# Prompt attention with values on column halves, and sample attention with cached rows turned by VectorE and scores on 16 tiles

## The chip, the core and the metric

The kernel runs on one core of one Trainium2 chip. The metric is the device time of one execution in microseconds (us); three runs were timed before. 

## The reference

One inference step of two decoder layers, in fp32, for 512 prompt tokens and for 8 sample sequences of 4 new tokens each, whose 4096 past positions lie in a paged cache. In each layer a combined projection feeds four branches; one of them is latent attention with 8 heads, a latent width of 128 and a rotary width of 32. Then come gates, a merge, a layer norm and a mixture of 16 experts. The part that matters here, shortened:

```python
def mla_attend(q_lat, q_rope, ckv, krope, q_pos, k_pos):
    s = einsum('bthc,blc->bhtl', q_lat, ckv) + einsum('bthr,blr->bhtl', q_rope, krope)
    s = where(q_pos >= k_pos, s * (QK_NOPE + QK_ROPE) ** -0.5, -1e30)
    return einsum('bhtl,blc->bthc', softmax(s, axis=-1), ckv)

lat = mla_attend(q_lat, q_rope, concat([past_ckv, ckv]), concat([past_krope, krope]), pos, k_pos)
c_out = einsum('bthc,chv->bthv', lat, w_uv)
```

For the samples the past keys are `cache_ckv[l, page_table]` (128 wide) and `cache_krope[l, page_table]` (32 wide).

## The kernel before

Each layer runs five stages one after the other, each a block with its own program for every engine: `project`, `attend` (prompt attention, behind a run of small products), `attend_sample`, `merge` and `experts`. Inside a block each engine works through its instructions in the order of the code and waits on semaphores; `due(k, sem, n)` is the count n of a semaphore within the layer. A new block starts when all engines have left the last one.

**`attend`.** The units of `B_UNITS` (L568) are small products on TensorE, each into one of four pairs of PSUM banks, and are taken from there by the engine named behind the colon (A ScalarE, D VectorE). The last, `qdr`, puts the rotary sample queries of 4 sequences on the diagonal of `qbd` (L779 to L784). Then 16 turns follow: a query block of 128 tokens (4) times a pair of heads (4). In turn i of block qb = i // 4, TensorE makes two score tiles over (qb + 1) x 128 keys (`scores`, L911, K = 96); VectorE adds the causal mask to the last 128 columns (L806), takes the maximum (L808) and makes the bias (L810); ScalarE takes the exponentials (L695). Two turns later TensorE turns the probabilities (`turn`, L938) and ScalarE copies them (L703); three turns later `values` (L928) multiplies, with the turned probabilities (128 columns) as the stationary side and 64 columns of V streaming. At the end of a block VectorE divides by the sums (`block_out`, L795), TensorE turns the 512 columns (`block_turn`, L944) and VectorE keeps them in `cc` (`block_keep`, L800). TensorE's order is scores(i), values(i-3), turn(i-2). Each fp32 product appears as two matmuls in the trace (two passes), a transpose as one.

**`attend_sample`.** 8 sequences are two halves of 4. A step s (of 8) is one half's 4 batches with 1024 keys each; partition r of a batch holds 8 consecutive cached rows. `load_cache` (L564, L565) fetches for each batch first the rotary rows (128 x 256) and then the latent rows (128 x 1024) by indirect DMA on GpSimd, with a semaphore each, into one of `BUFS` = 3 buffers. Steps 0 to 2 are loaded in `attend`. For the steps behind them the GpSimd program is:

```python
pool.wait_ge(*due(k, k.d_pv, 2 * (s - BUFS) + 2))
load_cache(k, pool, s, range(0, 2))
...
pool.wait_ge(*due(k, k.d_pv, 2 * (s - BUFS) + 3))
load_cache(k, pool, s, range(2, 4))
```

A step is worked in two units of 512 keys per batch. For a unit GpSimd lines up the rotary rows (L985); TensorE makes 4 transposes of them (L1010) and 16 of the latent rows (L1018), which VectorE and ScalarE copy out (L1137, L1140, L1098); then one rotary product with `qbd` and four latent products on column quarters (L1026, L1030) give the scores. VectorE takes the maximum (L1169 to L1173), ScalarE the exponentials (L1106); TensorE turns the probabilities (L1038), ScalarE copies them (L1114), and 32 matmuls on column quarters make the value product (L1047), after which `d_pv` counts one. VectorE adds it to the running output (L1153). TensorE's order is scores(u), values(u-1), turn(u+1), turn_probs(u). The new tokens' own keys are worked before unit 0 (L1055 to L1070, L1122 to L1146). SyncE fetches the first weights of `merge` once `d_pv` has reached 12. The stages that follow begin at L1254.

## Time and profile before

| | us |
|---|---|
| median of three runs | 1947.16 |
| lowest, highest | 1941.71, 1953.26 |
| span of the profiled execution | 1919.0 |
| its own total time | not recorded; the median is 28.2 above the span |
| TensorE busy | 1776.3 (93%) |
| VectorE busy | 801.3 (42%) |
| ScalarE busy | 444.7 (23%) |
| GpSimd busy | 372.1 (19%) |

Busy time is the time in which an engine had an instruction at work. TensorE's matmuls are pipelined, so a matmul's own length (for instance 0.60 us for 512 columns) is longer than the spacing of two of them. PEclk is the granted clock of TensorE as a share of 2.4 GHz; at 0.50 it is 1.2 GHz.

### The profile page before, as it was taken

How to read it: one execution, taken by the hardware profiler on the slowest of the kernel's cores; microseconds unless marked ns; L12 is line 12 of the kernel's file. 1: busy time of each engine (PE TensorE's matmuls, PEld its weight loads, DVE VectorE, ACT ScalarE, POOL GpSimd, SP SyncE). 2: the span in 40 equal slices, each digit the busy share in tenths (PEclk: the TensorE clock that was granted, in tenths of full speed). 3: DMA queues.
4: the chain of work that ended last, by engine and by line, in shares of the span. 5: the costliest groups of instructions: out<-in, count | busy, mean ns of one | idle time of the engine just before them, and what ended most of it. 6: DMA issues, size and time to landing. Idle time of an engine off the chain costs nothing. (4 is left out here: it accounts for less than half of the span.)

```text
span 1919.0 us, 24094 instructions
## 1 busy us (share of the span) xinstructions
PE 1776.3 (93%) x9428; PEld 1200.4 (63%) x9428; DVE 801.3 (42%) x1611; ACT 444.7 (23%) x949; POOL 372.1 (19%) x393
## 2 busy tenths in 40 slices
PE   8999899999999998999899988989999999999990
PEld 6877666788888454333378766657888874533330
DVE  4676455433333351111529654544333334511116
ACT  0125434211111121111310453431111111221111
POOL 0013045000000002364000230530000005024625
PEclk8998999999999989999999988999999999899995
DMA  9113136222223647995650140543212326689974
GB/s 275 59 33 111 32 102 202 94 88 87 78 67 110 254 196 300 417 413 228 242 154 1 58 117 1 155 149 121 88 61 83 104 81 272 263 350 414 416 276 167
DMA packets 141459, 322.40 MB, mean 168 GB/s; under 512 B 34862, under 2 KB 97060, under 8 KB 122852
## 3 DMA queue, kind: packets, MB, share of 16 engines
q1 hardware_dynamic: 103270, 204.45, 29.7%
q0 software_dynamic: 36576, 114.62, 16.9%
q10 hardware_dynamic: 1502, 1.80, 0.3%
q8 instruction: 76, 1.25, 0.3%
q14 instruction: 35, 0.29, 0.0%
HBM read 360.20 MB, written 29.48 MB: 203 GB/s over the span
## 5 line engine op out<-in xcount | busy, mean ns | idle before, releaser
L1240 PE MATMUL ps<-space 128*128 128x272 f32 x1024 | 250.3, 392 | 0.0
L1725 PE MATMUL ps<-space,xT 128*64 128x512 f32 x864 | 226.7, 595 | 0.0
L444 PE MATMUL ps<-xT,space 128*128 128x272 f32 (+1 forms) x960 | 225.4, 399 | 0.8 <-DMA space<-in_w_in 0.8
L1240 PEld LDWEIGHTS ps<-space 128*128 128x128 f32 x1024 | 194.6, 190 | 40.1
L444 PEld LDWEIGHTS ps<-xT,space 128*128 128x128 f32 (+1 forms) x960 | 184.0, 192 | 42.0 <-DMA space<-in_w_in 1.2
L1248 PE MATMUL ps<-space 128*128 128x272 f32 x640 | 157.1, 392 | 0.0
L1248 PEld LDWEIGHTS ps<-space 128*128 128x128 f32 x640 | 121.6, 190 | 25.1
L1986 DVE SCALAR_TENSOR_TENSOR space<-space,ps 128x256 f32<-128x256 f32 x32 | 21.5, 672 | 261.5 <-ACT space L1827 261.5
L1240 PE MATMUL ps<-xT,space 128*128 128x272 f32 x512 | 127.8, 392 | 0.0
L1725 PEld LDWEIGHTS ps<-space,xT 128*64 128x64 f32 x864 | 69.7, 137 | 90.7 <-issue 88.3
L1638 PE MATMUL ps<-space 128*128 128x512 f32 x256 | 115.8, 613 | 6.1 <-PEq L244 6.1
L1747 PE MATMUL ps<-space 128*64 128x512 f32 x512 | 115.4, 592 | 1.5 <-DVE space L1992 1.5
L1240 PEld LDWEIGHTS ps<-xT,space 128*128 128x128 f32 x512 | 97.3, 190 | 20.1
L531 DVE SCALAR_TENSOR_TENSOR space<-space,par 128x512 f32<-128x512 f32 x240 | 99.2, 495 | 0.0
L1638 PEld LDWEIGHTS ps<-space 128*128 128x128 f32 x256 | 49.9, 197 | 68.2 <-issue 68.2
L1345 DVE TENSOR_TENSOR space<-space 128x512 f32<-128x512 f32 x128 | 85.6, 688 | 2.3 <-DMA space<-in_w_in 0.2
L1018 PE MATMUL ps<-ident,space 128*128 128x128 f32 x512 | 73.0, 288 | 14.2 <-ACT space L1098 13.4
L1570 POOL DMA_DIRECT2D x_rows<-space x10 | 5.5, 550 | 409.6 <-DVE space L1885 409.6
L1747 PEld LDWEIGHTS ps<-space 128*64 128x64 f32 x512 | 36.6, 137 | 73.9 <-issue 71.9
L1355 DVE TENSOR_TENSOR space<-space,ps 128x544 f32<-128x544 f32 x48 | 34.6, 721 | 104.3 <-ACT space L1331 92.4
L1383 DVE TENSOR_TENSOR space<-space,ps 128x272 f32<-128x272 f32 x32 | 14.0, 439 | 152.3 <-ACT space L1325 152.3
L564 POOL DMA_INDIRECT space<-in_cache_krope,idx x64 | 62.4, 974 | 75.3 <-DMA space<-in_cache_ckv,idx 51.6
(381 smaller groups left out, 2494.1 us busy)
## 6 DMA issues: line engine op xcount, KB each, us to landing
space<-in_w_in SPq DMA_DIRECT2D x44, 1024.0 KB, 5.5
space<-in_exp_w_down SPq DMA_DIRECT2D x32, 1024.0 KB, 14.5
space<-in_exp_w_gate SPq DMA_DIRECT2D x30, 1024.0 KB, 10.7
space<-in_exp_w_up SPq DMA_DIRECT2D x30, 1024.0 KB, 12.8
space<-in_w_o SPq DMA_DIRECT2D x8, 1024.0 KB, 6.0
space<-x_rows SPq DMA_DIRECT2D x16, 512.0 KB, 6.1
space<-y_rows SPq DMA_DIRECT2D x16, 512.0 KB, 6.7
space<-in_p_attn SPq DMA_DIRECT2D x8, 512.0 KB, 6.5
```

The lines of the kernel that those rows point to most:

```text
L444: t = nc.tensor.matmul(ps[0:m, 2 * (n % 4) + h, 0:HN], w[:, f, c * P:c * P + m], k.xT[:, f, h, :], start=(f == 0), stop=(f == KD - 1))
L531: ch.step(v.scalar_tensor_tensor(dst, src, k.cw[:, c, tap:tap + 1], dst, ALU.mult, ALU.add))
L564: pool.indirect_dma_start(k.ckr[:, s % BUFS, b, :], None, k.kr_table, at).then_inc(k.c_inr[c], 16)
L1018: t = m.transpose(ps[:, b % 2, j * P:(j + 1) * P], k.ckv[:, s % BUFS, b, (4 * g + j) * P:(4 * g + j + 1) * P], k.ident[:])
L1240: t = m.matmul(out, w[:, f, :], x[:, f, :], start=(first and f == 0), stop=(f == H - 1), skip_group_check=True)
L1248: t = m.matmul(branch(mi)[:, h], w[:, f, mi * P:(mi + 1) * P], branches[b][:, f, h, :], start=(f == 0), stop=(f == BRANCH_TILES[b] - 1))
L1345: v.tensor_tensor(out, x, y, op).then_inc(k.e_s, 1)
L1355: v.tensor_tensor(g, g, p, ALU.mult).then_inc(k.e_t, 1)
L1638: t = m.matmul(ps[:, 2 * (i % 2) + half, :], merged[:, f, c:c + r], w[:, f % 2, 512 * half:512 * half + 512], start=(f == 0), stop=(f == K ...
L1725: i = m.matmul(ps[r, 6 + t % 2, :], k.xgT[:, t % 2, f, r], gate_up_of(g)[:, f], start=(f == 0), stop=(f == KD - 1), skip_group_check=True)
L1747: i = m.matmul(ps[r, half, :], k.hT[:, t % 2, j, r], down_of(g)[:, j, 512 * half:512 * half + 512], start=(j == 0), stop=(j == 1), skip_gr ...
L1986: v.scalar_tensor_tensor(h, g, k.wt[:, ORDER[t]:ORDER[t] + 1], u, ALU.mult, ALU.mult).then_inc(k.m_h, 1)
```

## The change

In prompt attention the values become the stationary side (64 columns, one head on each half of the output partitions) and the turned probabilities stream (128 columns), so the output arrives already turned. The division by the sums is applied by VectorE to the probabilities (`divide`), ahead of their transposes; `block_out` and `block_turn` go. A new unit `qrep` repeats the latent sample queries in 32-row blocks on all four partition quarters, and `qdr` is kept in the same layout; `qbd` and its memset go.

In sample attention a step is worked as one unit of 1024 keys. VectorE turns the cached rows in 32 x 32 blocks, five instructions of 128 x 1024 a step (`turn`). The scores are 5 blocks of 32 rows (four latent, one rotary), each on 4 row groups (one PSUM bank each) times 4 column quarters. The maximum and the exponential run over four banks of 256. Transposes of the probabilities, copies and value products are made in two halves g. GpSimd's line-ups go; its waits and loads stay. Some tiles move in memory, and semaphore counts follow.

```diff
@@ -675,6 +673,8 @@
             for c in range(2):
                 take(f"mix{c}")
                 taken(s.activation(k.aa[:, c], both(f"mix{c}"), ACT.Identity, scale=k.prm[:, 32 + c:33 + c]))
+            take("qrep")
+            taken(s.copy(k.qrep[:, 0:4].rearrange("p (h c) b n -> p h (c b n)", h=2), bank("qrep")))
...
+            i = v.tensor_tensor(k.qrep[:, 4].rearrange("p b (n t) -> p b n t", n=NH), bank("qdr")[:, 0, 0:256].rearrange("p (n b t) -> p b n t", n=NH, t=DS),
+                                k.rq[:, 4:36].rearrange("p (b t) -> p b t", t=DS)[:, :, None, :].broadcast_to([P, DB, NH, DS]), ALU.mult)
...
-            def block_out(qb):
-                dve.wait_ge(*due(k, k.c_exp, 8 * qb + 8))
-                n = 4 * qb
-                ch.step(v.reciprocal(k.rs[:, n:n + 4], k.sm[:, n:n + 4]))
+            def divide(i):
+                dve.wait_ge(*due(k, k.c_exp, 2 * i + 2))
+                ch.step(v.reciprocal(k.rs[:, i, :], k.sm[:, i, :]))
                 ch.settle()
-                dve.wait_ge(*due(k, k.c_v, n + 4))
-                if qb >= 2:
-                    dve.wait_ge(*due(k, k.c_ct, qb - 1))
-                v.tensor_tensor(k.oq[:, qb % 2].rearrange("p (n c) -> p n c", c=VH), ps[:, O + qb % 2, :].rearrange("p (n c) -> p n c", c=VH),
-                                k.rs[:, n:n + 4].rearrange("p i e -> p (i e)")[:, :, None].broadcast_to([P, NH, VH]), ALU.mult).then_inc(k.c_on, 1)
+                for e in range(2):
+                    p = k.prob[:, i % 3, e, 0:width(i)]
+                    v.tensor_scalar(p, p, k.rs[:, i, e:e + 1], None, ALU.mult).then_inc(k.c_on, 1)
 
             def block_keep(qb):
-                dve.wait_ge(*due(k, k.c_ct, qb + 1))
+                dve.wait_ge(*due(k, k.c_v, 4 * qb + 4))
                 v.tensor_copy(columns4(k.cc, qb), ps[:, O + qb % 2, :].rearrange("p (i n) -> p i n", i=4)).then_inc(k.c_cc, 1)
 
             for i in range(TURNS):
...
                 if i % 4 == 3 and i >= 7:
-                    block_out(i // 4 - 1)
-                if i % 4 == 1 and i >= 9:
-                    block_keep(i // 4 - 2)
+                    block_keep(i // 4 - 1)
...
                 halves(f"mix{c}", [(k.poolw[:, c, :], k.pooled[:, c])])
+            buffer("qrep")
+            pe.wait_ge(*due(k, k.b_D, b_taken("D", B_AT["ql"] + 1)))
+            for c in range(4):
+                t = m.matmul(bank("qrep")[:, c // 2, (c % 2) * 256:(c % 2 + 1) * 256], k.sel[:, c * P:(c + 1) * P], k.qs.rearrange("p b n -> p (b n)"), start=True, stop=True)
+            made(t)
...
-                for e in range(2):
-                    n = 2 * pair + e
-                    for b in range(qb + 1):
-                        t = m.matmul(ps[:, O + qb % 2, n * VH:(n + 1) * VH], k.probT[:, e, b * P:(b + 1) * P], k.vh[:, b, n * VH:(n + 1) * VH],
-                                     start=(b == 0), stop=(b == qb))
+                for b in range(qb + 1):
+                    for e in range(2):
+                        n = 2 * pair + e
+                        t = m.matmul(ps[VH * e:VH * e + VH, O + qb % 2, pair * P:(pair + 1) * P], k.vh[:, b, n * VH:(n + 1) * VH],
+                                     k.probT[:, e, b * P:(b + 1) * P], start=(b == 0), stop=(b == qb), skip_group_check=True)
                 t.then_inc(k.c_v, 1)
 
             def turn(j):
                 for e in range(2):
-                    pe.wait_ge(*due(k, k.c_exp, 2 * j + e + 1))
+                    pe.wait_ge(*due(k, k.c_on, 2 * j + e + 1))
                     if j >= 1:
                         pe.wait_ge(*due(k, k.c_pt, 2 * j - 1 + e))
                     for b in range(j // 4 + 1):
                         t = m.transpose(ps[:, T + e, b * P:(b + 1) * P], k.prob[:, j % 3, e, b * P:(b + 1) * P], k.ident[:])
                     t.then_inc(k.c_t, 1)
-
...
-            def line_up(u):
-                s, g = u // 2, u % 2
-                if g == 0:
-                    for b in range(4):
-                        pool.wait_ge(*due(k, k.c_inr[(s % BUFS) * 4 + b], 16 * (s // BUFS + 1)))
-                if u >= 2:
-                    pool.wait_ge(*due(k, k.d_krt, u - 1))
-                nc.gpsimd.tensor_copy(k.krl[:, g].rearrange("p j (b c) -> p b j c", b=4),
-                                      k.ckr[:, s % BUFS, :, g * P:(g + 1) * P].rearrange("p b (j c) -> p b j c", c=ROPE)).then_inc(k.d_krl, 1)
-
-            for u in range(4):
-                line_up(u)
             for s in range(BUFS, STEPS):
-                line_up(2 * s - 2)
                 pool.wait_ge(*due(k, k.d_pv, 2 * (s - BUFS) + 2))
                 load_cache(k, pool, s, range(0, 2))
-                line_up(2 * s - 1)
                 pool.wait_ge(*due(k, k.d_pv, 2 * (s - BUFS) + 3))
                 load_cache(k, pool, s, range(2, 4))
-            line_up(UNITS - 2)
-            line_up(UNITS - 1)
 
         @block.tensor
...
+            def scores(s):
+                h = s // LOADS
+                pe.wait_ge(*due(k, k.d_kr, s + 1))
+                pe.wait_ge(*due(k, k.d_kc, 4 * s + 4))
+                if s >= 1:
+                    pe.wait_ge(*due(k, k.d_exp, s))
+                for c in range(BLOCKS + 1):
+                    for i in range(4):
+                        for b in range(4):
+                            if c < BLOCKS:
+                                keys = k.kT[quadrant(i), s % 2, b, :].rearrange("p (j c n) -> p c j n", j=8, n=32)[:, c]
+                            else:
+                                keys = k.krT[s % 2][quadrant(i), b, :]
+                            t = m.matmul(ps[quadrant(b), i, 0:KEYS], k.qrep[quadrant(i), c, 4 * h + b, :], keys,
+                                         start=(c == 0), stop=(c == BLOCKS), skip_group_check=True)
+                t.then_inc(k.d_s, 1)
+
...
+            def turn_probs(s, g):
+                pe.wait_ge(*due(k, k.d_exp, s + 1))
+                if s >= 1:
+                    pe.wait_ge(*due(k, k.d_ptc, 2 * s + g - 1))
                 for j in range(4):
...
-            def values(u):
-                s, g = u // 2, u % 2
-                pe.wait_ge(*due(k, k.d_ptc, u + 1))
-                pe.wait_ge(*due(k, k.d_o, u + 1))
+            def values(s, g):
+                pe.wait_ge(*due(k, k.d_ptc, 2 * s + g + 1))
+                pe.wait_ge(*due(k, k.d_o, s + 1))
                 for j in range(4):
                     for b in range(4):
-                        t = m.matmul(ps[quadrant(b), V, 0:P], k.pT[:, u % 2, j, quadrant(b)], k.ckv[:, s % BUFS, b, (4 * g + j) * P:(4 * g + j + 1) * P],
-                                     start=(j == 0), stop=(j == 3), skip_group_check=True)
+                        t = m.matmul(ps[quadrant(b), V, 0:P], k.pT[:, g, j, quadrant(b)], k.ckv[:, s % BUFS, b, (4 * g + j) * P:(4 * g + j + 1) * P],
+                                     start=(g == 0 and j == 0), stop=(g == 1 and j == 3), skip_group_check=True)
                 t.then_inc(k.d_pv, 1)
...
-            for u in range(UNITS):
-                scores(u)
-                if u >= 1:
-                    values(u - 1)
-                if u + 1 < UNITS:
-                    turn(u + 1)
-                turn_probs(u)
-                if u == STEPS + 1:
+            scores(0)
+            for s in range(STEPS):
+                if s + 1 < STEPS:
+                    scores(s + 1)
+                for g in range(2):
+                    turn_probs(s, g)
+                for g in range(2):
+                    values(s, g)
+                if s == LOADS:
                     finish(0)
-            values(UNITS - 1)
             finish(1)
...
-                h, i = u // STEPS, u % STEPS
+            for u in range(STEPS):
...
+                    act.wait_ge(*due(k, k.d_pt, 2 * u - 2))
+                s.activation(k.prob2[:, u % 2, :].rearrange("p (j i n) -> p i j n", j=8, n=32), ps[:, 0:4, 0:KEYS].rearrange("p i (j n) -> p i j n", n=32),
+                             ACT.Exp, bias=k.nmx[:, h, i + 1:i + 2], scale=SCALE, accum_out=k.sums[:, h, i + 1:i + 2]).then_inc(k.d_exp, 1)
                 s.activation(k.fade[:, h, i:i + 1], k.mxs[:, h, i:i + 1], ACT.Exp, bias=k.nmx[:, h, i + 1:i + 2], scale=SCALE).then_inc(k.d_fade, 1)
-                if u + 1 < UNITS:
-                    keep(u + 1)
-                act.wait_ge(*due(k, k.d_pt, u + 1))
-                if u >= 2:
-                    act.wait_ge(*due(k, k.d_pv, u - 1))
-                s.copy(k.pT[:, u % 2].rearrange("p j n -> p (j n)"), ps[:, PT, :]).then_inc(k.d_ptc, 1)
+                for g in range(2):
+                    act.wait_ge(*due(k, k.d_pt, 2 * u + g + 1))
+                    if u >= 1:
+                        act.wait_ge(*due(k, k.d_pv, 2 * u + g - 1))
+                    s.copy(k.pT[:, g].rearrange("p j n -> p (j n)"), ps[:, PT + g, :]).then_inc(k.d_ptc, 1)
 
         @block.vector
...
+            def turn(s):
+                if s >= 2:
+                    dve.wait_ge(*due(k, k.d_s, s - 1))
+                for b in range(4):
+                    dve.wait_ge(*due(k, k.c_inr[(s % BUFS) * 4 + b], 16 * (s // BUFS + 1)))
+                v.transpose(k.krT[s % 2].rearrange("p b n -> p (b n)"), k.ckr[:, s % BUFS].rearrange("p b n -> p (b n)")).then_inc(k.d_kr, 1)
+                for b in range(4):
+                    dve.wait_ge(*due(k, k.c_in[(s % BUFS) * 4 + b], 16 * (s // BUFS + 1)))
+                    v.transpose(k.kT[:, s % 2, b, :], k.ckv[:, s % BUFS, b, :]).then_inc(k.d_kc, 1)
+
+            turn(0)
             dve.wait_ge(*due(k, k.d_sn, 1))
...
             v.tensor_copy(k.outs[:].rearrange("p h n -> p (h n)"), ps[:, V, 0:2 * P]).then_inc(k.d_o, 1)
+            turn(1)
...
+            for u in range(STEPS):
+                h, i = u // LOADS, u % LOADS
                 dve.wait_ge(*due(k, k.d_s, u + 1))
-                ch.step(v.reduce_max(k.top[:, u:u + 1], ps[:, S + u % 2, :], AX.X))
+                ch.step(v.tensor_reduce(k.top[:, u:u + 1], ps[:, 0:4, 0:KEYS], AX.XY, ALU.max))
                 ch.settle()
                 ch.step(v.tensor_tensor(k.mxs[:, h, i + 1:i + 2], k.mxs[:, h, i:i + 1], k.top[:, u:u + 1], ALU.max))
                 ch.settle()
                 v.tensor_scalar(k.nmx[:, h, i + 1:i + 2], k.mxs[:, h, i + 1:i + 2], -SCALE, None, ALU.mult).then_inc(k.d_m, 1)
                 if u >= 1:
                     gather_values(u - 1)
-                if u + 1 < UNITS:
-                    keep(u + 1)
+                if u + 2 < STEPS:
+                    turn(u + 2)
                 dve.wait_ge(*due(k, k.d_fade, u + 1))
                 ch.settle()
```

## Rows read from the trace of the kernel before

**Rows 1.** The page of the profile, its head and part 1.
```profile
span 1919.0 us, 24094 instructions
...
PE 1776.3 (93%) x9428; PEld 1200.4 (63%) x9428; DVE 801.3 (42%) x1611; ACT 444.7 (23%) x949; POOL 372.1 (19%) x393
```

**Rows 2.** Busy time by stretch; columns: us, engines, clock, DMA share, GB/s.
```profile
172.00:239.30 67.30, 57.42 (x320) 44.96 (x320) 29.43 (x60) 31.63 (x96) 9.53 (x11) 0.84 0.21 62
239.30:348.10 108.80, 96.90 (x1109) 65.85 (x1109) 59.18 (x143) 42.56 (x100) 47.83 (x56) 0.97 0.44 134
1118.00:1185.10 67.10, 57.11 (x320) 44.77 (x320) 29.51 (x60) 31.64 (x96) 9.45 (x10) 0.84 0.21 61
1185.10:1297.70 112.60, 98.26 (x1110) 67.19 (x1110) 59.11 (x143) 42.67 (x100) 47.84 (x56) 0.96 0.42 130
```

**Rows 3.** Timeline, one late prompt turn; columns: start us, us, engine, line, operation.
```profile
215.61 1.88 PE L916 MATMUL ps<-space 96*128 96x512 f32 x4
...
217.53 0.43 DVE L806 TENSOR_TENSOR ps<-ps,cmask 128x256 f32<-128x256 f32 x1 [1.73 <-PE ps L916]
...
219.53 0.78 ACT L695 ACTIVATE space<-ps,space 128x512 f32<-128x512 f32 x1 [1.90 <-DVE space L810]
...
221.05 1.07 ACT L703 COPY space<-ps 128x512 f32<-128x512 f32 x2
...
222.17 2.00 PE L928 MATMUL ps<-space 128*128 128x64 f32 x16 [0.34 <-ACT space L703]
...
224.01 1.05 PE L938 MATMUL ps<-ident,space 128*128 128x128 f32 x8
```

**Rows 4.** The timeline, sample attention, layer 1.
```profile
1207.01 1.06 PE L1047 MATMUL ps<-space 128*32 128x128 f32 x32
...
1207.26 0.69 DVE L1169 TENSOR_REDUCE space<-ps 128x1 f32<-128x512 f32 x1 [1.50 <-PE ps L1030]
...
1208.37 0.97 POOL L564 DMA_INDIRECT space<-in_cache_krope,idx  x1 [5.07 <-PE ps L1047]
1208.37 0.69 ACT L1106 ACTIVATE space<-ps,space 128x512 f32<-128x512 f32 x1 [2.41 <-DVE space L1173]
...
1209.65 0.94 POOL L565 DMA_INDIRECT space<-in_cache_ckv,idx  x1 [0.30 <-issue]
```

**Rows 5.** The timeline, end of prompt attention, layer 0.
```profile
237.06 0.69 DVE L795 TENSOR_TENSOR space<-ps,space 128x512 f32<-128x512 f32 x1 [5.37 <-issue]
...
238.50 0.69 DVE L800 COPY space<-ps 128x512 f32<-128x512 f32 x1 [0.75 <-PE ps L944]
```

**Rows 6.** Groups by line, 160 to 172 us; columns: busy us, mean ns.
```profile
L774 DVE COPY space<-ps 128x1024 f32<-128x1024 f32 x1 | 1.2, 1225 | 0.3 <-PE ps L886 0.3
L684 ACT COPY space<-ps 128x1024 f32<-128x1024 f32 x1 | 1.0, 1012 | 1.3 <-PE ps L886 1.3
```

**Rows 7.** Busy time by stretch, from sample attention into the merge, layer 0.
```profile
346.00:348.00 2.00, 0.64 (x13) 0.18 (x5) 1.00 (x4) 0.00 (x0) 0.00 (x0) 1.00 0.00 0
348.00:350.00 2.00, 1.79 (x18) 1.64 (x19) 1.72 (x2) 0.27 (x1) 0.00 (x0) 0.52 0.33 71
352.00:354.00 2.00, 2.00 (x10) 1.65 (x9) 2.00 (x3) 0.00 (x0) 0.00 (x0) 1.00 1.09 373
```

**Rows 8.** DMA issues by tensor, 259 to 340 us; the number: us to landing.
```profile
space<-in_cache_krope,idx POOLq DMA_INDIRECT x20, 3.6
space<-in_cache_ckv,idx POOLq DMA_INDIRECT x20, 4.7
```

**Rows 9.** The timeline, start and end of sample attention, layer 0.
```profile
240.44 0.17 DVE L1122 COPY space<-ps 128x16 f32<-128x16 f32 x1 [1.25 <-PE ps L1060]
...
246.90 0.42 DVE L1146 COPY space<-ps 128x256 f32<-128x256 f32 x1 [0.76 <-PE ps L1070]
...
345.23 1.08 PE L1047 MATMUL ps<-space 128*32 128x128 f32 x32 [0.68 <-ACT space L1114]
...
348.21 1.07 PE L1254 MATMUL ps<-space,wuv 128*64 128x32 f32 x16 [0.65 <-PEq L244]
```

More of the change, by code:

```diff
@@ L939, in turn @@
                     t.then_inc(k.c_t, 1)
-            def block_turn(qb):
-                pe.wait_ge(*due(k, k.c_on, qb + 1))
-                for i in range(4):
-                    t = m.transpose(ps[:, O + qb % 2, i * P:(i + 1) * P], k.oq[:, qb % 2, i * P:(i + 1) * P], k.ident[:])
-                t.then_inc(k.c_ct, 1)
             for i in range(TURNS + 3):
@@ L1021, in scores @@
-            def scores(u):
-                pe.wait_ge(*due(k, k.d_krc, u + 1))
-                if u >= 2:
-                    pe.wait_ge(*due(k, k.d_exp, u - 1))
-                half = u // STEPS
-                m.matmul(ps[:, S + u % 2, :], k.qbd[:, half, :], k.krT[:, u % 2, :], start=True, stop=False, skip_group_check=True)
-                pe.wait_ge(*due(k, k.d_kcA, 2 * u + 2))
-                pe.wait_ge(*due(k, k.d_kcD, 2 * u + 2))
-                for b in range(4):
-                    t = m.matmul(ps[quadrant(b), S + u % 2, :], k.qs[:, 4 * half + b, :], k.kT[:, u % 2, b, :], start=False, stop=True, skip_group_check=True)
-                t.then_inc(k.d_s, 1)
@@ L1033, in turn_probs @@
-            def turn_probs(u):
-                pe.wait_ge(*due(k, k.d_exp, u + 1))
-                if u >= 1:
-                    pe.wait_ge(*due(k, k.d_ptc, u))
-                for j in range(4):
-                    t = m.transpose(ps[:, PT, j * P:(j + 1) * P], k.prob2[:, u % 2, j * P:(j + 1) * P], k.ident[:])
+            def scores(s):
[14 more added lines that the diff above has]
+                t.then_inc(k.d_s, 1)
@@ L1059, in _ @@
                     m.matmul(out, k.qs[:, 4 * h + b, :], k.ckvT[:, h, HP:HN], start=True, stop=False, skip_group_check=True)
-                    t = m.matmul(out, k.qbd[:, h, quadrant(b)], k.krnew[:, h, :], start=False, stop=True, skip_group_check=True)
+                    t = m.matmul(out, k.qrep[0:32, BLOCKS, 4 * h + b, :], k.krnew[0:32, h, :], start=False, stop=True, skip_group_check=True)
             t.then_inc(k.d_sn, 1)
-            turn(0)
             pe.wait_ge(*due(k, k.d_pn, 2))
@@ L2123, in build @@
         k.lat = take(NH, 2, HS)
-        at = shared
-        k.oq = take(2, 512)
         at = shared + 4 * 2 * HN
```

97 lines of the change are left out of this document (29 added, 68 removed).

## The prediction

> **What bounds it now.** I read the page first: TensorE has work in 93% of a span of 1919.0 us [rows 1], so a change pays by shortening TensorE's queue or its waits. The table of stages [rows 2] then shows where the change acts. Prompt attention takes 67.3 us in layer 0 and 67.1 in layer 1, sample attention 108.8 us, 112.6 in layer 1. TensorE is occupied for 97 of 109 us of the sample stage, at nearly full clock, VectorE for 59.
>
> One late turn of the prompt loop [rows 3] shows a cycle over two turns: scores (1.88), mask, maximum and bias on VectorE (to 219.53), two exponentials (to 221.05), two copies (1.07), values (2.00), transposes (1.05). TensorE's own work is nearly as long. The 16 value matmuls take 2.00 us, some 0.12 apart, though each streams only 64 columns; I put that pace down to the loads of 128 columns of weights. Four matmuls of 512 columns take 1.88; with 0.60 for the last one they are 0.427 apart, so 256 would stream in 0.213 and 128 in 0.107.
>
> The profiled execution has a span of 1919.0 us; the median of the runs is 1947.16, 28.2 above it, for what lies around the span. I add the sum to both.
>
> **Prompt attention.** Values now load 64 columns and stream 128, and heads e = 0 and 1 go to different column halves. Quarters do run side by side: 32 matmuls of 128 columns end in 1.06 us [rows 4], where 8 rounds of 0.107 plus a latency of 0.2 make 1.06. I take the same for halves. The last block's values fall from 16 x 0.117 = 1.87 to 8 x 0.107 = 0.86, a saving of 0.25 us for each key block of a turn. Turns 0 to 12 have 28 such blocks, 7 us; half of it counts where the two-turn cycle sets the pace, 3.5 us. The tail is one chain: three values save 3 x 1.0, and the last normalisation, its four transposes and their waits go (237.06 to 238.50, 1.4 [rows 5]), as do the four of the block before, about 0.8. Together 5.2. The divisions move onto VectorE ahead of the transposes: a reciprocal and two 128x512 multiplications a turn, bounded between 0.6 and 1.6 us from the 0.69 of a 128x512 operation [rows 5]. VectorE works 2.0 of some 4.3 us there, and a transpose comes a turn behind its exponential, so I cost them at nothing; without that cover they would add up to 1.6 x 16. The new unit for the repeated queries adds 8 matmuls of 256 columns, 1.7 us, to a stretch where TensorE is the pace, and a copy of 1.0 us [rows 6] beside them. The final four small multiplications become one, -0.5. Sum: -3.5 - 5.2 + 1.7 - 0.5 = -7.5, with the rounding of waits **-8 us a layer** (-3 to -13: less if TensorE's clock falls as it is busy less).
>
> **Sample attention: what goes.** 16 units with 20 TensorE transposes each, their copies and GpSimd's line-ups. What comes on VectorE: five 128x1024 transposes a step. No row has one. The nearest, a VectorE copy of 128x1024, takes 1.23 us [rows 6]; a 128x512 operation at 0.69 has the same pace. I take 1.25, 6.3 a step. The bounds are half and double (0.6 and 2.4), since a plain copy says nothing of what 4-byte blocks cost to turn. The Trainium skill (Vector Engine (DVE) Microarchitecture Reference, section 3.8) gives one element per cycle and lane, at which 1024 elements would pass at about the pace of that copy; no row here shows it.
>
> Scores: 5 blocks x 16 tiles x 2 passes = 160 matmuls of 256 columns. Side by side on 16 tiles they stream in 10 x 0.213 = 2.1 us; at the pace of the small matmuls, 0.027 each [rows 4], they need 4.3. With the latency of 0.2 that is 2.3 to 4.5. I take 4.0, near the upper end, because each burst will probably begin at the lower of the two levels (1.2 GHz, where 256 columns take twice as long): from 346 to 348 TensorE was occupied for 0.64 of 2 us, from 348 to 350 its granted clock was 0.52, and from 352 to 354, at work again, 1.00 [rows 7]. The Trainium skill (TensorE: Matmul & The Clock Gate, Part 1, Wait — 56ns, not 53.3ns?) has a floor of about 25 ns from start to start for small matmuls. By it the 160 would need 4.0 whatever the clock, where streaming alone says 2.1; the trace of before does not decide, as streaming alone explains their 27 ns.
>
> **The wait that decides.** GpSimd's load of later steps stays as written: the diff leaves GpSimd's waits as they were. Batches 2 and 3 of step s are fetched once d_pv reaches 2(s-3)+3. Before, that was the next half step; now it is the first value product of step s-2. So with u = s-2, VectorE stands in turn(u+2), in front of the maximum of u+1, until: exp(u), scores(u+1), probability transposes, values(u,0), four indirect DMAs. Before, VectorE had no such wait and the loads had time to spare. Steps 3 to 7 all have it, so five periods, from one values(u,0) to the next, are:
> - GpSimd's reaction 0.3, and the issue of the third DMA of the half 2.5 later (0.97 + 0.3 + 0.94 + 0.3) [rows 4];
> - landing of that rotary part 3.6 us from its issue [rows 8], and 0.15 to react. The latent part of batch 3, issued 1.3 later and 4.7 on its way [rows 8], lands while the others are turned;
> - turn 6.3, the update of the sum 0.25;
> - maximum and bias: 1.11 for 512 elements [rows 4] plus 0.53 for 512 more, 1.65;
> - exponential of 1024: the copy's 1.01 [rows 6] plus accumulation and hand-over, 1.35 (two of 512 took 1.52 [rows 3]);
> - scores 4.0, since scores(u+2) stand ahead of the transposes in TensorE's queue;
> - four transposes 0.6, their copy 0.65, values 1.1.
>
> Sum 22.45 us, **five periods 112.3**. Bounds: 17.5 with fast transposes and fast scores, 24.3 with every TensorE term at half clock.
>
> Ahead of them: turn(0) 6.3 with nothing beside it, the new-token part 4.2 (before 6.9 [rows 9], of which 2.7 waited for transposes that go), turn(1) 6.3, maximum 1.65, turn(2) 6.3, the sum 0.25, maximum 1.65, exponential 1.35, scores 3.5, then 2.35 to the end of values(1,0): 33.9. Behind the last: the second half, 0.85, transposes and copy 1.25, values 1.95, then 1.9 as now to the next stage [rows 9], and some hand-overs: 6.6. With 0.3 of entry the stage takes 153.1 us, +44.3 in layer 0 and +40.5 in layer 1. The total is 44.3 + 40.5 - 16 = **+69 us**: a span of 1988, and 1947.2 + 69 = **2016 us**. The weights that SyncE fetches for the next stage wait for step 5 and have over 20 us left, so they cost nothing.
>
> **Rivals.**
> - *The loads are hidden after all* (the other side). Place: turn(3) to turn(7). If what they need had landed, the pace would be VectorE's 8.8 us, or GpSimd's issue of eight DMAs, 4 x 2.52 = 10.1 [rows 4], which is longer. Then 33.9 + 50.5 + 6.9 = 91.3: -17.5 and -21.3 in the sample stages, with -16 a total of -55, 1892. It decides below a period of about 15 us, where the stage is as long as now plus what the prompt gives. For it: VectorE is 54% busy, and the removal of so much TensorE work is real. Against it: the chain above closes on itself through a semaphore, and no overlap breaks it. 9%.
> - *Fast transposes*, 0.6 each: 3.2 less in each of eight turns, 51 us in two layers, 1965. 10%.
> - *Row groups take turns*: no row shows two row groups at work together, so the 16 tiles may run as four at a time. Then scores take 40 x 0.213 + 0.2 = 8.7, 4.7 more for each of about six exposed steps, +57: 2073. The Trainium skill (TensorEngine Tiling (Array Packing), Key Properties) says that tiles operate independently, the reading by which I priced them. 9%.
> - *Slow transposes*, 2.4 each: 5.8 x 8 x 2 = +93, 2109. 7%.
> - *The shorter work and the new waits cancel*: a period of 15 us, 1947. Nothing in the rows gives that period; 3%.
>
> **How the numbers follow.** The forecast has 62%; its own range, from the clock and landing terms, is 1990 to 2045. The range 1960 to 2078 takes in fast transposes and serial row groups, and leaves out 19%. About 0.5% (10 us) is what a measurement of this kernel can tell from no change. Faster: the hidden loads, 0.09. Within 0.5%: 0.03. Slower: the other four, 0.88.
>
> **What would show it.** In the profile of the changed kernel: VectorE's transposes of the rotary rows wait some 12 us in five steps a layer for the krope DMA; the second half's DMAs start right after values(u,0); steps 3 to 7 are about 22 us apart; TensorE's granted clock in the sample stage drops well under 0.97; the prompt stage is shorter by 8. The forecast is wrong if those waits are absent, if a transpose is not near 1.25 us, or if the 160 score matmuls do not end within about 4 us.

## The result, and the profile after

The changed kernel takes 2025.11 us (median of 4 runs, 2023.10 to 2028.83), the kernel before on the same chip 1947.68: a ratio of 1.0404, 95% interval 1.0373 to 1.0435. It is slower, by 77.4 us.

Chips of two paces appear in what follows, and they have to be kept apart. B stands for those on which the kernel before takes 1944 to 1948 us: there the runs above were made and the changed kernel's profile below (the record names no chip for these), and the last four experiments (chip 1). A stands for those on which it takes 1919 to 1921 us: there the first eight experiments ran (four on chip 7, four on chip 10). The profile of before has a span of 1919.0 and products of 37.2 us (from the first small product of `attend` to the first score matmul of the prompt), as e1 on A has them, while the median of 1947 is B's. The changed kernel's profiled execution took 2028.83 us with a span of 2027.0, so only 1.8 us lie around a span, not 28.2.

The head of the page of the changed kernel, then its busy time by stretch (us, PE, PEld, DVE, ACT, POOL, clock, DMA share, GB/s): prompt and sample attention of layer 0, then of layer 1.

```profile
span 2027.0 us, 26820 instructions
...
PE 1720.3 (85%) x11012; PEld 1155.6 (57%) x11012; DVE 828.0 (41%) x1591; ACT 401.7 (20%) x839; POOL 352.7 (17%) x359
```

```profile
179.80:238.40 58.60, 46.27 (x298) 29.84 (x296) 38.71 (x101) 31.49 (x96) 9.52 (x10) 0.85 0.23 68
238.40:400.70 162.30, 73.27 (x1909) 52.77 (x1910) 63.96 (x95) 20.39 (x44) 37.84 (x40) 0.68 0.29 90
1177.70:1237.10 59.40, 46.06 (x305) 29.92 (x305) 38.85 (x101) 31.49 (x96) 9.53 (x10) 0.89 0.23 69
1237.10:1400.90 163.80, 74.50 (x1909) 53.74 (x1910) 63.98 (x95) 20.47 (x44) 37.82 (x40) 0.69 0.29 90
```

Against [rows 2], TensorE works 24 us less in a sample stage, as the change means it to. But the stage is 53.5 us longer in layer 0 (51.2 in layer 1), and no engine is busy for even half of it. The prompt stage, measured from its first score matmul to the first instruction of sample attention, goes from 67.4 and 67.5 to 59.6 and 59.4.

One late prompt turn, to be held against [rows 3]:

```profile
219.83 0.88 DVE L789 TENSOR_SCALAR space<-space 128x512 f32<-128x512 f32 x2
...
220.38 1.88 PE L914 MATMUL ps<-space 96*128 96x512 f32 x4
...
222.20 0.88 PE L926 MATMUL ps<-space 128*64 128x128 f32 x12
...
223.01 1.09 PE L936 MATMUL ps<-ident,space 128*128 128x128 f32 x8
```

The value products of three key blocks take 0.88 us (sixteen matmuls for four blocks take 1.09, where they took 2.00), and the two divisions 0.88 on VectorE, which still waits 1.59 us for the scores behind them.

Now one period of the sample stage in layer 0, in the timeline of the changed kernel:

```profile
299.02 1.95 PE L1009 MATMUL ps<-space 128*32 128x128 f32 x64 [0.24 <-ACT space L1066]
300.40 0.95 POOL L564 DMA_INDIRECT space<-in_cache_krope,idx  x1 [12.48 <-PE ps L1009]
...
302.90 0.95 POOL L564 DMA_INDIRECT space<-in_cache_krope,idx  x1 [0.30 <-issue]
...
306.41 1.25 DVE L1078 STREAM_TRANSPOSE space<-space 128x1024 f32<-128x1024 f32 x1 [14.46 <-DMA space<-in_cache_krope,idx]
...
307.57 4.58 DVE L1081 STREAM_TRANSPOSE space<-space 128x1024 f32<-128x1024 f32 x4
...
312.17 1.22 DVE L1122 TENSOR_REDUCE space<-ps 128x1 f32<-128x1024 f32 x1
...
313.81 1.11 ACT L1059 ACTIVATE space<-ps,space 128x1024 f32<-128x1024 f32 x1 [14.36 <-DVE space L1126]
...
315.16 5.43 PE L992 MATMUL ps<-space,fifth 32*32 32x256 f32 x160 [14.19 <-ACT space L1059]
...
320.52 1.09 PE L1001 MATMUL ps<-ident,space 128*128 128x128 f32 x8
...
321.86 1.41 PE L1009 MATMUL ps<-space 128*32 128x128 f32 x44 [0.24 <-ACT space L1066]
```

Every line follows from the one above it, in its engine's queue or by a semaphore, and the last is the first again, one step later: values, rotary load, landing, turn, maximum, exponential, scores, turned probabilities, values. The five steps that wait so for their rows, 3 to 7, are called starved in what follows. The list of waits has VectorE's for layer 0 in one line (us in total, times, longest), 16 us a step where the forecast had some 12:

```profile
DVE space L1078 <- DMA space<-in_cache_krope,idx: 80.8, 5, 18.0
```

### The profile page after: what moved, and what is told of

It reads as the page before. It is cut to its first block and busy times, and to the rows that moved or that the text cites. A ratio compares the mean times of both kernels' runs of the same rounds, so it can differ in the third digit from the quotient of the medians.

```text
span 2027.0 us, 26820 instructions
## 1 busy us (share of the span) xinstructions
PE 1720.3 (85%) x11012; PEld 1155.6 (57%) x11012; DVE 828.0 (41%) x1591; ACT 401.7 (20%) x839; POOL 352.7 (17%) x359
## 3 DMA queue, kind: packets, MB, share of 16 engines
q1 hardware_dynamic: 103270, 204.45, 28.2%
## 5 line engine op out<-in xcount | busy, mean ns | idle before, releaser
L992 PE MATMUL ps<-space,fifth 32*32 32x256 f32 x2560 | 89.1, 581 | 161.5 <-ACT space L1059 150.2
L444 PEld LDWEIGHTS ps<-xT,space 128*128 128x128 f32 (+1 forms) x960 | 182.8, 191 | 41.5 <-DMA space<-in_w_in 1.3
L992 PEld LDWEIGHTS ps<-space,fifth 32*32 32x32 f32 x2560 | 57.6, 131 | 186.5 <-issue 168.2
L1591 PEld LDWEIGHTS ps<-space 128*128 128x128 f32 x256 | 49.3, 195 | 67.5 <-issue 67.5
L1078 DVE STREAM_TRANSPOSE space<-space 128x1024 f32<-128x1024 f32 x16 | 19.9, 1244 | 164.9 <-DMA space<-in_cache_krope,idx 163.8
```

What stands on the lines that cost most here:

```text
L444: t = nc.tensor.matmul(ps[0:m, 2 * (n % 4) + h, 0:HN], w[:, f, c * P:c * P + m], k.xT[:, f, h, :], start=(f == 0), stop=(f == KD - 1))
L992: t = m.matmul(ps[quadrant(b), i, 0:KEYS], k.qrep[quadrant(i), c, 4 * h + b, :], keys, start=(c == 0), stop=(c == BLOCKS), skip_group_chec ...
L1591: t = m.matmul(ps[:, 2 * (i % 2) + half, :], merged[:, f, c:c + r], w[:, f % 2, 512 * half:512 * half + 512], start=(f == 0), stop=(f == K ...
```

## The experiments

**On A, chip 7: four edits of the code beside each other** (before: 1920.67 us). `e1_prompt_alone` puts only the prompt part into the kernel before. The other three start from the changed kernel.

```diff
 # e2_one_wait, in the GpSimd program
 pool.wait_ge(*due(k, k.d_pv, 2 * (s - BUFS) + 2))
-load_cache(k, pool, s, range(0, 2))
-pool.wait_ge(*due(k, k.d_pv, 2 * (s - BUFS) + 3))
-load_cache(k, pool, s, range(2, 4))
+load_cache(k, pool, s)
 # e3_rotary_early, the same place
+pool.wait_ge(*due(k, k.d_kr, s - BUFS + 1))
+load_cache(k, pool, s, parts="r")
+pool.wait_ge(*due(k, k.d_pv, 2 * (s - BUFS) + 2))
+load_cache(k, pool, s, parts="c")
 # e4_no_loads: steps 3 to 7 are not loaded; they work on the rows of steps 0 to 2
```

> The prompt part of the change alone, with sample attention as it was before. If the prompt stage's saving (67 to 59.5 us a layer in the trace of the changed kernel) is its own and nothing gives it back, the time is 15 to 16 us below the kernel before, about 1932 us, a ratio of 0.992. If the saving only came from the new layout of the tiles or is lost in the sample stage behind it (a colder TensorE), the time stays within 5 us of before.

Measured: 1902.05 us, ratio 0.990 (0.9871 to 0.9928), the prompt stages 59.7 and 59.6 us. The prompt part saves 7.7 and 7.9 us of these stages by itself, and the kernel is 18.6 us faster; the 3 us more than two stages give lie within the interval.

> The changed kernel, but all four batches of a step are fetched once the last value product of the step that held the buffer is done, with no second wait for the step behind it. Theory of the late loads: the wait for the rotary rows loses one of its two steps, a period falls from 23.4 to about 15 us, five periods in each of two layers, so about 85 us come back: 1940 us. Rival, that the period is made of VectorE's transposes and TensorE's score matmuls and the load would be late anyhow for the issue of eight DMAs: less than 20 us come back, above 2005 us.

Measured: 1932.95 us, ratio 1.0065 (1.0045 to 1.0086); sample stages 121.8 and 122.0 us. VectorE's waits:

```profile
DVE space L1076 <- DMA space<-in_cache_krope,idx: 39.4, 5, 11.8
```

The exponentials of steps 2, 4 and 6 start at 280.52, 309.76 and 339.74 us: the loop now closes over two steps, 29.2 and 30.0 us long, so a step costs about 15; the first of the five is still 21.2 and the last 19.7 long, and their mean is 16.1. Against the changed kernel on A (e5 below) 69.5 us come back, of the 85 expected; the rival's 20 are exceeded by far.

> The changed kernel, with the rotary rows of step s fetched as soon as VectorE has turned those of step s-3, and the latent rows behind the last value product of step s-3. Theory of the late loads: the rotary rows no longer stand in the path; what is left is four latent DMAs (the last issued after 3.8 us and landing 4.7 later), one transpose, maximum, exponential, scores, transposes and values, 22.5 us for two steps, so 11.3 a step: about 1903 us, faster than both kernels. If GpSimd's ten microseconds of issue for a step set the pace, about the same (10.1 to 11). Rival: above 2000 us.

Measured: 1898.58 us, ratio 0.9879 (0.9842 to 0.9916); sample stages 108.3 and 105.6 us. That is 103.9 us under the changed kernel on A (e5); the forecast, counted from B's 2025, had 122, with 11.3 us a step where the five took 13.3 in the mean. No wait for rotary rows is left in the list; this one takes their place:

```profile
DVE space L1083 <- DMA space<-in_cache_ckv,idx: 20.1, 15, 3.3
```

> The changed kernel without the loads of steps 3 to 7; those steps work on the rows that the buffers hold from steps 0 to 2, so their part of the cache is left out. What remains is the pace of the engines: scores 5.3, transposes and values 4.1 on TensorE are 9.4 us a step, VectorE 8.3. Theory of the late loads: about 1880 us. Rival (transposes and scores are the cost themselves): above 1990 us. If the nine microseconds that scores took while loads ran in the second step come from those loads, every score burst now takes 4.7 to 5.6 us.

Measured: 1859.26 us, ratio 0.9678 (0.9637 to 0.972); sample stages 84.4 and 86.2 us. That is what the new arithmetic costs when no cache row is late: 24 and 26 us a layer under the kernel before, and 143 us in all under the changed kernel on A (forecast, from 2025 to 1880: 145).

**On A, chip 10: the order, and the changed kernel itself** (before: 1919.46 us).

> The changed kernel itself, so that its stages stand beside those of its variants. Both theories expect a ratio of 1.04 to the kernel before and sample stages of 162 to 164 us. They differ on the products ahead of the prompt stage, which took 43.9 and 45.0 us in the changed kernel's own profile and 38.4 in three variants: if the 5.5 us more belong to the change's code (the product with 4 x 256 columns and its copies), they stand here again; if they belong to that execution's memory traffic, the products take 38.4 us here and the span is about 11 us shorter against the kernel before.

Measured: 2002.46 us, ratio 1.0437 (1.0405 to 1.047); sample stages 157.4 and 156.4 us, products 38.4 us in both layers. So the products' 43.9 and 45.0 us of the profile above are not the change's code by itself: the same code takes 5.5 to 6.6 us less on A. In the sample stage the periods are about the same (22.7 us), but the burst of scores in the second step (the third burst) is whole here, 3.62 us long, where it took 9.47 on B.

```diff
 # e6_scores_last, TensorE's order; e7_early_and_last is the same on e3
 for s in range(STEPS):
-    if s + 1 < STEPS:
-        scores(s + 1)
     for g in range(2):
         turn_probs(s, g)
     for g in range(2):
         values(s, g)
+    if s + 1 < STEPS:
+        scores(s + 1)
```

> Only TensorE's order is changed: the turns of the probabilities and the values of step s come ahead of the scores of step s + 1. My theory: in the changed kernel the scores of the next step lie between the exponential and the values for which GpSimd's second wait holds, so they are in the period of 23.4 us with their 4.6 to 5.6 us; put behind the values they run while the cache rows are loaded. Period 18.0 to 18.8 us, five of them, sample stage 137 to 142 us instead of 163, kernel 45 to 52 us faster than the changed one. The rival, that the period is the queue's (issue and landing of eight loads with a compute chain beside them), expects the period to stay within 1 us of 23.4 and the kernel within 5 us of the changed one.

Measured: 1985.61 us, ratio 1.0353 (1.032 to 1.0385), 17 us faster than the changed kernel where 45 to 52 were expected. The stages are 149.4 and 147.6 us. A period of its timeline:

```profile
300.60 1.11 ACT L1059 ACTIVATE space<-ps,space 128x1024 f32<-128x1024 f32 x1 [15.24 <-DVE space L1126]
...
301.86 1.97 PE L1001 MATMUL ps<-ident,space 128*128 128x128 f32 x8 [10.34 <-ACT space L1059]
...
303.76 2.46 PE L1009 MATMUL ps<-space 128*32 128x128 f32 x64
...
305.66 0.95 POOL L564 DMA_INDIRECT space<-in_cache_krope,idx  x1 [9.06 <-PE ps L1009]
306.15 3.50 PE L992 MATMUL ps<-space,fifth 32*32 32x256 f32 x160
...
308.15 0.95 POOL L564 DMA_INDIRECT space<-in_cache_krope,idx  x1 [0.30 <-issue]
...
313.06 1.25 DVE L1078 STREAM_TRANSPOSE space<-space 128x1024 f32<-128x1024 f32 x1 [12.20 <-DMA space<-in_cache_krope,idx]
```

The period from exponential to exponential is 19.87 us (300.60 to 320.47), against 22.66 in the changed kernel (304.01 to 326.67). Of that, 4.7 us are the scores, and 1.9 come back. Without a burst of scores ahead of them, the turned probabilities and the first values run at the lower clock, from 301.8 to 303.8 granted 0.50 of the full one: 1.90 us from the first turn to the values instead of 1.33, and 1.90 instead of 1.38 from there to the load, 1.1 together. The landing, from the load's start to VectorE's transpose, is 7.40 instead of 6.55, 0.85 more. Over the five starved steps the gain is 15.9 us, but the first step took 11.8 instead of 8.7 and the last 11.5 instead of 7.7, since nothing lies beside their maximum and exponential. The scores were in the period, as the theory said; its price for taking them out was wrong.

> The rotary rows loaded as soon as VectorE has turned those of their buffer, the latent rows after one wait, and the scores behind the values. My theory: the loop over two steps is 2 x 13.3 us with the early rotary rows alone; without the scores of about 4.7 us in it, it is 21.9, or 11 a step, and then the chain within one step (scores 4.7, maximum 1.65, exponential 1.35, turns 0.6, copy 0.65, values 2 to 2.3, and 0.5 in between: 11.5) is as long. Period 11.3 to 12.2, stage 97 to 102 us instead of 108.3 and 105.6, kernel 9 to 20 us faster than with the early rotary rows alone (ratio 0.978 to 0.984 to the kernel before). The rival, that GpSimd's descriptors and the gaps in TensorE's issue while loads run set the 13.3 us, expects no gain, or up to 5 us slower, since the scores no longer lie beside the maximum of another step.

Measured: 1899.66 us, ratio 0.9898 (0.9874 to 0.9922), no faster than e3. The stages are 105.8 and 106.1 us. The period is 11.6 us (six steps in 69.5), inside the forecast, and the waits for cache rows are all but gone (0.4 us in layer 0), so the rival is wrong about the period. The period fits the forecast's chain within one step, 11.5 us. Against e3 the five middle steps gain 9.2 us (57.4 against 66.6), and the first and last lose 2.2 and 3.4, for want of cover as in e6. That leaves 3.6 us where the forecast, which did not count the ends, had 4 to 11; 2.4 stand in layer 0 and nothing in layer 1.

```diff
 # e8_early_two_waits, on e3: the latent rows after the two waits of the changed kernel
 pool.wait_ge(*due(k, k.d_pv, 2 * (s - BUFS) + 2))
-load_cache(k, pool, s, parts="c")
+load_cache(k, pool, s, range(0, 2), parts="c")
+pool.wait_ge(*due(k, k.d_pv, 2 * (s - BUFS) + 3))
+load_cache(k, pool, s, range(2, 4), parts="c")
```

> The rotary rows loaded early, but the latent rows after the same two waits as in the changed kernel. My theory: landing of the rotary rows and their turn leave the period, and four issues of rotary rows, but the second pair of latent rows still waits for the first half of the values of the step before. Period about 17 (0.3 + two issues 1.2 to 2.5 + landing 4.7 + last turn 1.2 + maximum 1.65 + exponential 1.35 + scores 4.7 + turns and copy 1.3 + first half of values 1.1), stage 128 to 134 us, kernel 55 to 68 us faster than the changed one and 10 to 22 slower than the kernel before. The rival, that the wait for the rotary rows is the whole loss and the two waits cost nothing by themselves, expects a period near 13.3 and the kernel faster than the one before by 1%.

Measured: 1960.92 us, ratio 1.0224 (1.0192 to 1.0255), 41.5 us faster than the changed kernel; stages 136.3 and 136.5 us, period 19.1 in the mean. The rival is wrong: with rotary rows early, the second wait alone costs 62 us against e3. The period was undervalued by 2 us: most of that is a slip in adding, since the terms listed make 17.5 to 18.8, not 17, and the score bursts took 4.7 to 5.8 us instead of 4.7.

**On B, chip 1** (before: 1944.48 us).

> As in the run without the loads of steps 3 to 7, and each of the 160 score matmuls of a step streams 64 of its 256 columns, so three quarters of the scores are left out. Theory 1 (the 16 tiles overlap fully and what is left is the issue of 160 matmuls, about 23 ns each): the burst stays at 3.5 to 3.9 us at the full clock. Theory 2 (streaming sets it): with a quarter of the columns it falls from 3.6 to about 1 to 2 us. In either case 4.6 to 5.6 us at the lower clock would have to stay at 4.6 or more if it is issue, and fall under 3 if it is streaming.

The kernel leaves out three quarters of the score columns. One execution was timed, 1867.12 us; what counts is its trace. Its bursts and, below them, those of e4 (on A) with all columns, each pair first at the lower clock (granted 0.50) and then at the full one:

```profile
258.18 2.39 PE L989 MATMUL ps<-space,fifth 32*32 32x64 f32 x160 [6.84 <-DVE space L1075]
...
292.17 1.78 PE L989 MATMUL ps<-space,fifth 32*32 32x64 f32 x160 [0.56 <-ACT space L1056]
```

```profile
251.80 5.59 PE L989 MATMUL ps<-space,fifth 32*32 32x256 f32 x160 [3.93 <-DVE space L1075]
...
260.69 3.38 PE L989 MATMUL ps<-space,fifth 32*32 32x256 f32 x160
```

So streaming sets the burst: 64 columns instead of 256 take 1.60 us off at the full clock and 3.20 at the lower one. Worked out to all 256 columns that is 2.13 and 4.27 us, the ten rounds of 0.213 of the forecast, and about 1.3 us are left at either clock. Issue at 25 ns each is ruled out: 160 matmuls in 1.78 us are 11 ns apart.

```diff
 # e10_late_fill, SyncE in attend_sample; e11_early_late_fill is the same on e3
 sp.wait_ge(*due(k, k.d_pv, 2 * (STEPS - BUFS) + 2))
+sp.wait_ge(*due(k, k.d_kr, STEPS))
 fill_branch(k, l, sp, 0, 0)
```

> The changed kernel, and SyncE's first two weight transfers of the merge (256 KB and 1 MB), which the values of step 5 release together with the last cache rows, wait for the turn of the last rotary rows as well. In the changed kernel the last starved step takes 26.3 us and the four before it 21.6 to 23.6, since its rotary rows land 9.1 us after the release where the others need 6.5. My theory: the two transfers share the DMA engines with the last rows; without them the last step takes 23.5 to 24, the stage is 2 to 3 us shorter in each layer, the merge still gets its weights in time, and the kernel is 4 to 6 us faster than the changed one (ratio about 1.041). The rival, that the landing of the last rows is long by itself (no following loads keep the queue going), expects the last step to stay at 26, and the merge, if anything, later by up to 3 us a layer.

Measured: 2019.93 us, ratio 1.0396 (1.036 to 1.0432); against the changed kernel's 1.0404 the difference is within the intervals. The profiles show the mechanism at a smaller size: the last starved step takes 23.55 us (361.23 to 384.78 in the exponentials) instead of 25.39, and its rotary rows are turned 4.75 us after their issue instead of 6.66. The two weight transfers do crowd the last rows, for 1.8 us a layer where 2 to 3 were forecast; in the whole kernel that does not show. 4.75 is still more than the 3.51 of the period above, so they are not all of it.

> The early rotary rows with one wait for the latent rows, and the merge's first weights late as in the run before. In the version without the late weights VectorE waited 4.3 us for the latent rows of the last step, 5.8 and 3.3 us for those of two steps before. My theory: the last step is 1 to 3 us shorter, the kernel 2 to 5 us faster than without (ratio 0.985 to 0.987). The rival expects no difference, or a merge that starts late by up to 3 us a layer (ratio up to 0.991).

Measured: 1967.23 us, ratio 1.0121 (1.0095 to 1.0147), where e3 on A had 0.9879. Both theories are wrong, and not because of the weights. The starved steps before the last take 18.8 to 20.0 us, in code that is e3's up to there; sample stages 132.0 and 133.0 us. In its timeline TensorE's burst of scores in the second step looks like this; below it is the one burst of e3 in that layer that has a gap:

```profile
264.47 4.31 PE L995 MATMUL ps<-space,fifth 32*32 32x256 f32 x65
...
269.12 0.63 PE L995 MATMUL ps<-space,fifth 32*32 32x256 f32 x4 [0.35 <-issue]
...
270.55 0.62 PE L995 MATMUL ps<-space,fifth 32*32 32x256 f32 x4 [0.80 <-issue]
...
272.00 2.50 PE L995 MATMUL ps<-space,fifth 32*32 32x256 f32 x7 [0.83 <-issue]
...
275.55 4.04 PE L995 MATMUL ps<-space,fifth 32*32 32x256 f32 x80 [1.05 <-issue]
```

```profile
274.34 4.21 PE L994 MATMUL ps<-space,fifth 32*32 32x256 f32 x123 [7.53 <-ACT space L1061]
280.78 1.94 PE L994 MATMUL ps<-space,fifth 32*32 32x256 f32 x37 [2.23 <-issue]
```

On B the burst takes 15 us instead of 3.4 to 5.6, broken by gaps in which TensorE waits for nothing that the profile shows, and they fall where GpSimd's cache loads are in flight. In e3, on A, there is one gap a layer, of 2.2 and 1.5 us. The changed kernel has such gaps too, on B, in the one burst of each layer that runs beside loads (265.74 to 275.2 us, 9.5 instead of 3.6), and none on A. Its other bursts start after the loads have landed, sheltered by the wait. Once the wait is gone, as in e3 and e11, bursts and loads overlap.

```diff
 # e12_mixed_order, on e11
 for s in range(STEPS):
+    ahead = s in (0, STEPS - 2)
-    if s + 1 < STEPS:
+    if ahead:
         scores(s + 1)
     ...
+    if not ahead and s + 1 < STEPS:
+        scores(s + 1)
```

> As the run before, with the scores of the next step behind the values for steps 1 to 5, and ahead of the turns, as in the changed kernel, for steps 0 and 6. With the scores last everywhere the steps had a period of 11.6 us and no waits for loads, 12.6 us with the scores first; but the first and last step took 11.1 and 12.1 us instead of 8.9 and 8.7, since nothing lay beside the maximum and the exponential. My theory: mixed, both gains stand: 8.9 + 5 x 11.6 + 8.8 us, the sample stage 99 to 102 us (106 with either order), the kernel 7 to 14 us faster than the run before (ratio 0.978 to 0.983). The rival, that with the scores ahead in step 0 the loads and the gaps in TensorE's issue come back over the whole stage, expects a stage of 104 to 108 us and a ratio within 0.002 of the run before.

Measured: 1988.15 us, ratio 1.0233 (1.0204 to 1.0262); stages 145.9 and 146.4 us. The rival expected the gaps back but no loss against e11, so it too was short: with the scores behind the values, nothing covers the gaps. The second step's burst lasts from 272.47 to 291.15 us, and its exponential starts behind it, at 292.83. What this order gives on A was not measured.

## Why the prediction was right, and where its steps were not

- **Direction and mechanism: right, and shown.** VectorE stands in front of the rotary rows in five steps a layer, as forecast, and the chain closes through GpSimd's second wait. Removing that wait alone gives back 69.5 us (e2 against e5), loading the rotary rows early gives 41.5 (e8), the two together 103.9 (e3), and taking the loads away 143 (e4), each on A against e5.
- **The period: 22.45 forecast, 22.84 in the period shown**, by terms. Values to load 1.38 (1.1 + 0.3), issue 2.50 (2.50), landing and reaction 3.51 (3.75), turn and sum update 5.76 (6.55), maximum and bias 1.64 (1.65), exponential 1.35 (1.35), scores 5.36 (4.0), turned probabilities and copy 1.34 (1.25). That close a sum holds in part by luck: the turn was 0.8 too high and the scores 1.4 too low.
- **The turn: right.** The transposes last 1.20 to 1.25 us against 1.25; four in a row take 4.58. The rivals of fast and slow transposes are out. The Trainium skill (Vector Engine (DVE) Microarchitecture Reference, section 3.8) has one element per cycle and lane, and the trace agrees as far as a pace tells it: 1024 elements of 4 bytes in 1.20 to 1.25 us, a copy's 1.23.
- **The scores: the mis-sized term.** Forecast 4.0, measured 4.6 to 5.7 in the starved steps, at a granted clock of 0.53 to 0.68 (three bursts of layer 0). The reason given (starts at the lower clock) was right; what failed is the upper bound, 160 matmuls at the 27 ns of [rows 4]. It left the lower clock out of the streaming, and 27 ns is no limit of the issue. By the forecast's own sign (bursts that do not end within about 4 us) this step was wrong. The Trainium skill (TensorE: Matmul & The Clock Gate, Part 1) has a floor of about 25 ns from start to start, and e9 has 11 ns on the 16 tiles. Streaming plus 1.3 us would have given 3.4 at the full clock and 5.6 at half.
- **Row groups in turn: out.** 160 matmuls in 3.38 us, where 8.7 would be needed. The tiles run side by side, as the Trainium skill (TensorEngine Tiling (Array Packing), Key Properties) says.
- **The stage: 153.1 forecast, 162.3 measured on B and 157.4 on A.** What lies outside the five periods came out as summed: 40.8 forecast, 40.95 on B (162.3 less 121.35, from the exponential at 264.36 to that at 385.71), with 1 us less ahead of the five than the terms give and 1 more behind them. All of the miss is in the five periods, 121.35 against 112.3 (116.89 on A), and two of them make most of it. The first of them took 27.3 us, with the gaps in TensorE's issue. The last took 25.4, where the forecast said that SyncE's weights "cost nothing": they were in time for the merge but in the way of the last cache rows, 1.8 us (e10).
- **The loads hidden: the rival on the other side.** No version has its stage of 91.3 us: it is 84.4 with no loads at all, and 105.7 with all of them in the fastest stage measured (e3). Its point of decision, a period of 15 us, is about right: e2, with 16.1 in the mean, is 0.7% slower than before.
- **Prompt: forecast -8, measured -7.8 and -8.0 on B (against the profile of before, which is of A's pace), -7.0 and -7.2 on A**, but these are without the new unit of repeated queries, which the forecast had inside its -8. That unit shows as 1.2 us more in the products on A (38.4 against 37.2), so the net on A is -5.8 and -6.0 and the gain was overstated by 2 us a layer.
- **The bookkeeping: wrong, without harm.** The 28.2 us that the forecast saw "around the span" are, but for 1.8, what fits the difference between A and B. On A the sum of +69 met +83.0, on B +77.4: 14 and 8 us too little. On A the sample stages explain 7.6 of it and the prompt part 4.3; 2 are spread over the other stages. For B no profile of before exists, so its share by stage stays unknown.

**Two kinds of gaps in TensorE's issue.** The isolated ones stand at the same places of the instruction stream on both kinds of chip: in e2 and e3 (chip 7) and in e9 (chip 1) behind matmul 121 to 123 of a burst or behind matmul 142 to 145. In e9, where no cache load is under way, the fourth burst breaks where that of e3 does, and in the same stretch (275.3 to 277.3 us) the list of queues has one packet, of instructions:

```profile
274.42 1.79 PE L989 MATMUL ps<-space,fifth 32*32 32x64 f32 x123 [3.66 <-ACT space L1056]
278.12 0.87 PE L989 MATMUL ps<-space,fifth 32*32 32x64 f32 x37 [1.91 <-issue]
```

```profile
q8 instruction: 1, 0.02, 3.8%
```

All nine such gaps of the three runs (0.3 to 2.2 us) have a packet of 16 KB on that queue beside them, and in all nine TensorE goes on 1.3 to 1.6 us after the packet has ended. So what these gaps wait for is, as far as a trace can tell, the supply of instructions, with cache loads or without. The many gaps of e11's bursts are of another kind: that of 264.47 has no packet of instructions from 265.2 to 277.3 us, while the cache rows move.

**What stays open.** Why bursts beside cache loads break in many places on B and not on A. The loads are needed for it: the changed kernel's bursts that start after the loads are whole on B too, and e9, without the loads and with 64 columns, has the isolated gaps only. The products' 5.5 us on B, again beside the loads of step 0, look different once more. TensorE's rows start as on A up to the 60th matmul, yet ScalarE gets the results up to 4.95 us later; the next matmul starts 3.7 us late, and eight at the lower clock lose the rest. What holds the results back is not visible. That e11 differs from e3 by the chip and not by its one added wait is argued from the steps before that wait; e3 itself did not run on B, nor did e1.

## What to carry to other kernels

When a stage is cut into larger steps, recount every wait that a buffer's release hangs on: here two half-steps became one, an unchanged line of GpSimd's program turned from a slack wait into a loop, and a stage whose engines alone need 84 us took 157. Draw the loop from release to release and time its links before moving work to an idle engine. Where the loads are moved forward, look next at what then runs beside them, and measure on more than one chip: e3 was 1.2% faster than before on chip 7, and the same code up to its last starved step 1.2% slower on chip 1. Of these versions the prompt part alone is the one to keep (0.990 on A), since it leaves the loads and waits of the sample stage as they were; whether it also holds on B was not measured.

## What the runs showed of the hardware

- A VectorE transpose of 128x1024 in fp32, in 32x32 blocks, takes 1.20 to 1.25 us, a copy's pace.
- 160 fp32 matmuls on 16 tiles of 32x32: about 1.3 us plus 2.13 for streaming 256 columns at the full clock, 4.27 at half; down to 11 ns from start to start with 64 columns (e4, e9).
- The clock follows what TensorE did just before: taking a 4.7 us burst out of the way made the turned probabilities and the values behind it 1.1 us slower, at a granted clock of 0.50.
- TensorE seems to run out of instructions inside bursts of small matmuls: gaps of 0.3 to 2.2 us that ended 1.3 to 1.6 us after a 16 KB packet of the instruction queue, at the same matmul on different chips (e2, e3, e9).
- One program, different chips: the kernel before takes 1919.46 us on chip 10 and 1944.48 on chip 1, 1.3% more; the products of the changed kernel take 5.5 to 6.6 us a layer more on B, and a burst of small matmuls beside indirect loads lasts 15 us in e11 and 8.4 at most in e3.
